# Attention scores written head by head instead of matmul kind by matmul kind

## The reference

```
sc = einsum('bqhd,bkhd->bhqk', qi, k) * scale
sc = sc + (cum_q - cum_k)            # cum: running sum of log forget gates
sc = where(kpos <= qpos, sc, -inf)
```

```
sc = (einsum('bqhd,bkhd->bhqk', qn, k_nope)
      + einsum('bqhr,bkr->bhqk', qr, k_rope)) * scale
sc = where(visible, sc, -inf)
```

## Time and profile before

| | us |
|---|---|
| median of 3 runs | 3754.56 (3749.29 to 3756.58) |
| the profiled execution, its own time | 3749.29 |
| its span, first to last instruction | 3747.4 |
| PE busy | 3166.1 (84% of the span) |
| DVE busy | 2247.1 (60%) |
| ACT busy | 1429.8 (38%) |
| mean granted clock of PE | 0.934 of full speed |

### The profile page before, as it was taken

How to read it: one execution, slowest core, us unless ns; L and a number is a source line. 1 busy time by engine, 2 the same in 40 slices (tenths; PEclk the granted TensorE clock), 3 DMA queues, 4 the chain that set the end, 5 groups by cost and what they waited for, 6 DMA issues and landing times. The chain is left out here.

```text
span 3747.4 us, 46785 instructions
## 1 busy us (share of the span) xinstructions
PE 3166.1 (84%) x15952; PEld 2087.9 (56%) x15952; DVE 2247.1 (60%) x5038; ACT 1429.8 (38%) x3564; POOL 962.4 (26%) x796
## 2 busy tenths in 40 slices
PE   3886999999988999897766798888877989889897
PEld 2774566554444655442345644444326779777897
DVE  5664766667667666679414466767752259512397
ACT  1222444434334444443224244444432237423275
POOL 0001433434333333344200155444550000000000
PEclk7887999999999999999977899999998989899999
DMA  6746999999999999999967499999992235332353
GB/s 248 277 167 267 418 415 417 421 419 409 421 420 399 409 405 415 415 417 352 369 230 238 163 421 421 421 421 415 415 406 106 90 130 179 135 115 91 129 183 118
DMA packets 177136, 1152.67 MB, mean 308 GB/s; under 512 B 21860, under 2 KB 30264, under 8 KB 43306
## 3 DMA queue, kind: packets, MB, share of 16 engines
q0 software_dynamic: 113936, 827.38, 53.9%
q1 hardware_dynamic: 56058, 304.90, 21.6%
q10 hardware_dynamic: 6944, 17.91, 1.3%
HBM read 1128.86 MB, written 21.25 MB: 307 GB/s over the span
## 5 line engine op out<-in xcount | busy, mean ns | idle before, releaser
L1126 PE MATMUL PS<-AR 128*128 128x512 f32 x3072 | 1511.9, 618 | 249.6 <-ACT AR L1184 241.7
L1311 POOL DMA_INDIRECT AR<-in_peer_uv,AR x768 | 949.2, 1236 | 1514.0 <-PE PS L1126 1109.2
L1287 DVE CUSTOM_DVE_ANT_0 AR<-AR,H 128x1024 f32<-128x1024 f32 x768 | 940.9, 1225 | 655.9 <-DMA AR<-in_peer_uv,AR 636.2
L1126 PEld LDWEIGHTS PS<-AR 128*128 128x128 f32 x3072 | 559.8, 193 | 852.9 <-issue 420.4
L1179 ACT ACTIVATE SM<-SM 128x1 f32<-128x1 f32 x768 | 155.7, 203 | 1130.4 <-DVE SM L1287 1125.3
L1087 PEld LDWEIGHTS PS<-HT,W 128*128 128x128 f32 x1536 | 298.9, 195 | 273.2 <-issue 258.0
L1087 PE MATMUL PS<-HT,W 128*128 128x256 f32 x1536 | 427.6, 387 | 2.7 <-issue 1.3
L1184 ACT ACTIVATE AR<-CON,SM 128x128 f32<-128x128 f32 x768 | 309.1, 402 | 45.6 <-PE PS L1126 21.1
L2578 PE MATMUL PS<-XP,WP 128*128 128x256 f32 x2112 | 264.2, 287 | 22.5 <-DVE WP L2735 15.4
L2578 PEld LDWEIGHTS PS<-XP,WP 128*128 128x128 f32 x2112 | 261.0, 196 | 28.2 <-issue 27.7
L1181 ACT ACTIVATE SM<-SM 128x1 f32<-128x1 f32 x768 | 227.1, 296 | 25.1
(11 more groups left out here) (368 smaller groups left out, 3313.0 us busy)
## 6 DMA issues: line engine op xcount, KB each, us to landing
W<-in_peer_w_q SPq DMA_DIRECT2D x48, 1024.0 KB
W<-in_ada_w SPq DMA_DIRECT2D x32, 1024.0 KB
W<-in_ffn_gate SPq DMA_DIRECT2D x22, 1024.0 KB
W<-in_ffn_val SPq DMA_DIRECT2D x22, 1024.0 KB
W<-in_ffn_out SPq DMA_DIRECT2D x22, 1024.0 KB
W<-in_cm_w_in SPq DMA_DIRECT2D x16, 1024.0 KB
AR<-min_scr SPq DMA_DIRECT2D x16, 1024.0 KB, 9.6
AR<-in_peer_uv,AR POOLq DMA_INDIRECT x768
```

The costliest lines, as they stand in the source:

```text
L1126: mm = pe.matmul(PS[:, 4 + (u % 2) * 2 + c, :], self.DIAG[:, r % 4, :], self.UV[:, r % RING, D + c * 512:D + (c + 1) * 512], start=(k == 0 ...
L1287: v.tensor_tensor_reduce(rows_, rows_, H[:, self.tb(u), :], 1.0, 0.0, ALU.mult, ALU.add, self.ACTV[:, u % 2, k:k + 1]).then_inc(u_used.sem, 1)
L1311: g.indirect_dma_start(out=self.UV[:, r % RING, :], out_offset=None, in_=t["peer_uv"], in_offset=bass.IndirectOffsetOnAxis(ap=self.IDS[:, ...
```

## The change

The same matmuls are issued in another order. In fox all five matmuls of head 0 now come before the five of head 1. In mla all six matmuls of a head come together, and the wait for `o_taken` stands at the head of each of the four, with the same value. In mla `att_sums` is still raised once for each head, now as each is finished. The lines are renumbered: fox 2409, 2411, 2413, 2415, 2416 become 2410 to 2414; mla 2906 and 2910 become 2907 and 2909.

```
-for i, h in enumerate(heads):
-    pe.matmul(PS[:, 3 + i, 0:P], QP[h, s, 0:P], KP[h, s, 0:P], ...)
-for i in range(2):
-    pe.matmul(PS[:, 3 + i, 0:P], LT[:, i, 0:P], SUF[:, 0, 0:P], ...)
-for i, h in enumerate(heads):
-    pe.matmul(PS[:, 3 + i, P:SCORES], QP[h, s, P:SEQ], KP[h, s, :], ...)
 for i in range(2):
-    pe.matmul(PS[:, 3 + i, P:SCORES], LT[:, i, P:SEQ], SUF[:, 0, :], ...)
-    mm = pe.matmul(PS[:, 3 + i, P:SCORES], LT[:, i, SEQ:SCORES], SUF[:, 1, :], ...)
+    h = slice(i * FOX_D, (i + 1) * FOX_D)
+    first, second = PS[:, 3 + i, 0:P], PS[:, 3 + i, P:SCORES]
+    pe.matmul(first, QP[h, s, 0:P], KP[h, s, 0:P], ...)
+    pe.matmul(first, LT[:, i, 0:P], SUF[:, 0, 0:P], ...)
+    pe.matmul(second, QP[h, s, P:SEQ], KP[h, s, :], ...)
+    pe.matmul(second, LT[:, i, P:SEQ], SUF[:, 0, :], ...)
+    mm = pe.matmul(second, LT[:, i, SEQ:SCORES], SUF[:, 1, :], ...)
...
-pe.wait_ge(o_taken, BY_ROWS + 1 + r * (2 * G4))
-for (lo, hi), q in zip(PIECES, (slice(0, P), slice(P, SEQ))):
-    keys = slice(0, hi - lo)
-    for i in range(G4):
-        pe.matmul(PS[:, i, lo:hi], QN[:, i, q], KN[:, i, keys], ...)
-    for x in range(2):
-        for i in range(G4):
-            b = slice(i * 32, (i + 1) * 32)
-            mm = pe.matmul(PS[:, i, lo:hi], QR[b, x, q], KR[b, x, keys], ...)
-            if lo and x:
-                mm.then_inc(att_sums, 1)
+for i in range(G4):
+    pe.wait_ge(o_taken, BY_ROWS + 1 + r * (2 * G4))
+    b = slice(i * 32, (i + 1) * 32)
+    for (lo, hi), q in zip(PIECES, (slice(0, P), slice(P, SEQ))):
+        keys = slice(0, hi - lo)
+        out = PS[:, i, lo:hi]
+        pe.matmul(out, QN[:, i, q], KN[:, i, keys], ...)
+        for x in range(2):
+            mm = pe.matmul(out, QR[b, x, q], KR[b, x, keys], ...)
+    mm.then_inc(att_sums, 1)
```

More of the change, by code:

```diff
@@ L2406, in scores @@
                     pe.wait_ge(s_taken, 1 + j * 2)
-                    heads = [slice(i * FOX_D, (i + 1) * FOX_D) for i in range(2)]
-                    for i, h in enumerate(heads):
-                        pe.matmul(PS[:, 3 + i, 0:P], QP[h, s, 0:P], KP[h, s, 0:P], start=True, stop=False)
                     for i in range(2):
-                        pe.matmul(PS[:, 3 + i, 0:P], LT[:, i, 0:P], SUF[:, 0, 0:P], start=False, stop=True)
-                    for i, h in enumerate(heads):
-                        pe.matmul(PS[:, 3 + i, P:SCORES], QP[h, s, P:SEQ], KP[h, s, :], start=True, stop=False)
-                    for i in range(2):
-                        pe.matmul(PS[:, 3 + i, P:SCORES], LT[:, i, P:SEQ], SUF[:, 0, :], start=False, stop=False)
-                        mm = pe.matmul(PS[:, 3 + i, P:SCORES], LT[:, i, SEQ:SCORES], SUF[:, 1, :], start=False, stop=True)
+                        h = slice(i * FOX_D, (i + 1) * FOX_D)
+                        first, second = PS[:, 3 + i, 0:P], PS[:, 3 + i, P:SCORES]
+                        pe.matmul(first, QP[h, s, 0:P], KP[h, s, 0:P], start=True, stop=False)
+                        pe.matmul(first, LT[:, i, 0:P], SUF[:, 0, 0:P], start=False, stop=True)
+                        pe.matmul(second, QP[h, s, P:SEQ], KP[h, s, :], start=True, stop=False)
+                        pe.matmul(second, LT[:, i, P:SEQ], SUF[:, 0, :], start=False, stop=False)
+                        mm = pe.matmul(second, LT[:, i, SEQ:SCORES], SUF[:, 1, :], start=False, stop=True)
                     mm.then_inc(att_sums, 1)
@@ L2901, in scores @@
                     pe.wait_ge(roped, r + 1)
-                    pe.wait_ge(o_taken, BY_ROWS + 1 + r * (2 * G4))
-                    for (lo, hi), q in zip(PIECES, (slice(0, P), slice(P, SEQ))):
-                        keys = slice(0, hi - lo)
-                        for i in range(G4):
-                            pe.matmul(PS[:, i, lo:hi], QN[:, i, q], KN[:, i, keys], start=True, stop=False)
-                        for x in range(2):
-                            for i in range(G4):
-                                b = slice(i * 32, (i + 1) * 32)
-                                mm = pe.matmul(PS[:, i, lo:hi], QR[b, x, q], KR[b, x, keys], start=False, stop=(x == 1))
-                                if lo and x:
-                                    mm.then_inc(att_sums, 1)
+                    for i in range(G4):
[4 more added lines that the diff above has]
+                            out = PS[:, i, lo:hi]
+                            pe.matmul(out, QN[:, i, q], KN[:, i, keys], start=True, stop=False)
+                            for x in range(2):
+                                mm = pe.matmul(out, QR[b, x, q], KR[b, x, keys], start=False, stop=(x == 1))
+                        mm.then_inc(att_sums, 1)
                 def values(r):
```

## The result

The changed kernel took 3823.83 us (median of 4 runs, 3813.0 to 3828.56) against 3753.47 for the kernel before. The ratio is 1.0176, with a 95% interval from 1.0152 to 1.0200. The forecast was 3787 (3776 to 3802): the direction was right, but the loss is 70 us, where the forecast sum had 35. Over all 13 of its executions the changed kernel lies between 3805.67 and 3832.92, with a median of 3819.04.

What follows compares the result with a forecast made beforehand. PE was taken as the bound, with the scores fully on the path: fox +11.4, mla +24.9, early masks -1.4, sum +34.9 us. On two bases this gave 3784.2 and 3789.5; forecast 3787, range 3776 to 3802.

Steps and rivals of the forecast that it cites:

- What bounds the stages: Fox and mla loops: PE bounds them, DVE and ACT are hidden behind the projection, so time PE loses in scores is lost.
- Rival D: Fox and mla: the scores leave the path, so longer scores cost nothing; 3747.9 us, no change; chance 0.03.
- the 4.2 us before L2434: Fox loop: read as the only wait there, 4.2 us over seven pairs, for a copy of ACT.
- The pace of the scores: Fox and mla scores: record and row-change costs give 4.95 us a fox pair (+11.4) and 2.745 a mla head (+24.9).
- only the first round of mla lacks a row change at its start: Mla scores: the first round lacks that row change both before and after, so its difference is the same.
- Rival C: Fox and mla scores: weights can't load at a row place while a matmul runs there; 23 us more, 3807; chance 0.04.
- The masks that DVE does early: Last mla round: DVE masks heads 0 to 2 during the scores, shortening PE's 3.84 us wait by 1.4 us.
- The hoped-for higher clock in these transposes: Last mla round: a shorter wait may keep the clock up, between 0 and -1.5 us; taken as 0.
- The added waits for `o_taken`: Mla scores: the three added waits a round cost nothing, or 0.6 us in all at the upper end.
- The clock: Scores of fox and mla: granted clock stays 1.00, since PE would never stand idle there; no time added.
- rival A: Mla scores: lone 32-row groups drop the clock to 1.2 GHz; 23.6 us more, 3808, up to 3815; chance 0.08.
- The size of rival A: Mla: 1.97 us more a slow head, 12 heads, 23.6 us; up to 3815 if projection starts are slow too.

Runs made afterwards that it cites:

- rows128: The changed kernel with each lone rotary matmul of mla on all 128 rows, so no row change is left in mla: 3787.23 us.
- fox_only: The kernel before with only the fox scores in the changed order, mla left as before: 3773.89 us, ratio 1.0058.

## Why the prediction was wrong

- What bounds the stages: right. No new wait came up in the loops, and what was lost in the scores was lost by the kernel. Rival D is out. One reading was off without effect: the 4.2 us before L2434 are of six pairs of fox, and a seventh adds 0.6.
- The pace of the scores (0.1125 and 0.215 us a record, 0.19 to 0.20 a row change, other row places free): right. 4.95 us a pair and 2.74 a head were measured wherever the clock was at 1.00. Its remark that only the first round of mla lacks a row change at its start is wrong: 128-row matmuls stand before every round. The later rounds are 0.11 us longer with no row change in the kernel as well (`rows128`, 7.97 and 7.86 us). It did no harm, since both kernels have it.
- Rival C, weight loads that wait for a matmul at the same place: out. A lone group of four 32-row records took 0.64 us, which leaves no room for four loads of 0.184 in series with the matmuls. The Trainium skill (TensorE: Matmul & The Clock Gate, Part 3, What overlaps and what doesn't) says that a weight load overlaps with matmuls in flight only when the row group differs; these traces do not agree with it.
- The masks that DVE does early: right in size. PE's wait before the last round's transposes fell from 3.84 to 2.39 us, by 1.45 with 1.4 forecast, as this row of the changed kernel shows, which answers to the last of the earlier trace rows:

```profile
3511.22 3.54 PE L2917 MATMUL PS<-CON,AR 128*128 128x128 f32 x12 [2.39 <-ACT AR L2968]
```

The hoped-for higher clock in these transposes did not come: from their start to the first product they take 3.33 us, and 3.32 before.
- The added waits for `o_taken`: no cost seen. The idle time before L2907 is the 2.5 us of before.
- The clock: wrong, and this is the step that failed. The forecast put the clock's term at nothing, 1.00 through the scores, and gave rival A 0.08, on the ground that PE would never stand idle there. In the run PE did not stand idle, and the clock fell all the same, to 0.53 over 3366 to 3375: 23.8 us in the score stretches and 5.8 us in the projections behind them. The evidence was read too widely: the stretch at 1.00 had four 32-row groups side by side, that is all 128 rows at work, and told nothing of a lone one. The range of the forecast ended at 3802, short of the rival's own 3808 to 3815.
- The size of rival A. For mla it was about right, by two errors that partly cancel: a slow head costs 5.02 - 2.74 = 2.28 us more, not 1.97, since the row changes also get slower; and seven of the 16 heads ran slow throughout and four in part (17.4 / 2.28, some 8 heads' worth), not 12. So the 17.4 us stand against the rival's 23.6. The slow start of the three projections behind them gave 5.8, against the 7 of its upper end. What it left out is fox: lone 64-row matmuls were not thought of as a risk, and in four profiled executions out of five with this order of fox two or three pairs of eight ran slow (6.4 us in the changed kernel, 9.2 in `fox_only`). Why these pairs and not the others isn't shown.

## What to carry to other kernels

Matmuls that use part of the array's rows should stand in groups that fill the rows together, for two reasons: they run side by side for about the time of one, and in these runs the granted clock then stayed up. Order them so that the number of rows in use changes as seldom as possible, even across pieces. When a change leaves PE busy but makes it use less of its array, put the clock among the main cases and not among the remote ones.

## What the runs showed of the hardware

- The granted clock fell from 2.4 to 1.2 GHz in a stream in which PE never paused, when its matmuls used 32 of 128 rows (0.69 over a round); the same stream on 128 rows kept 1.00. With the lone ones on 64 rows and wide ones between, three rounds of four kept it, and in fox two or three pairs of eight lost it in four of five profiled executions. Which measure of the array's use decides, and where its limit lies, these runs don't say.
- A change of the row count costs 0.19 to 0.20 us at the high clock. At the low clock it costs more. The slow head of 5.02 us has four such changes; its records at double their pace are 3.94, which leaves 0.27 us a change.
- The spread of the times is larger where the clock falls: 13 executions of the changed kernel cover 27.3 us, 23 of the kernel before 13.0 us. That the clock is the reason isn't shown.
